# A two-layer hybrid decoder step: the next tile's input projections dealt over other steps of a slot, with second buffers for heads and turned x

## The reference, cut to what matters

```python
for each layer:
    xn = rmsnorm(x, norm_mix)
    (a_gate, a_x, b_q, b_k, b_v, b_qi, b_ki, b_wi, c_q, c_k, c_v, c_g, c_a) = split_cols(xn @ w_in)   # 2644 columns
    y_a = rglru_mixer(a_gate, a_x, ...)               # convolution of 4, gates, linear recurrence over rows
    q, k = rope(rmsnorm(b_q)), rope(rmsnorm(b_k))     # 8 query heads, 4 key heads of 64
    y_b = sparse attention: index scores from b_qi, b_ki, b_wi; the best 256 keys of each row; softmax over these
    y_c = gla_mixer(c_q, c_k, c_v, c_g, c_a, ...)     # gated linear attention with a state S
    x = x + concat(y_a, y_b, y_c) @ w_out
    x = x + square(relu(rmsnorm(x, norm_mlp) @ w_up)) @ w_down
```

## Time and profile before

| what | value |
|---|---|
| time, median of 3 runs | 4064.79 us (4063.27 to 4065.57) |
| span of the profiled execution (the page gives no other time for it) | 4072.7 us |
| busy in the span: PE, DVE, ACT, POOL | 88%, 52%, 25%, 12% |
| granted PE clock, mean | 0.89 of full speed |
| prompt mixer, layer 0 | about 36 to 990 us |
| prompt mixer, layer 1 | about 2057 to 3010 us |

### The profile page before, as it was taken

One profiled execution on the slowest core, in us unless ns is written; L12 is line 12 of the kernel. 1 busy time (PEld: TensorE's weight loads), 2 busy tenths in 40 slices (PEclk: granted clock), 3 DMA queues, 4 the chain that ended last, 5 costly groups with the idle time before them and its releaser, 6 DMA issues.

```text
span 4072.7 us, 52249 instructions
## 1 busy us (share of the span) xinstructions
PE 3569.3 (88%) x17850; PEld 2698.7 (66%) x17850; DVE 2124.8 (52%) x4881; ACT 1018.2 (25%) x2269; POOL 474.9 (12%) x637
## 2 busy tenths in 40 slices
PE   5778778888799999999987787787787999999999
PEld 3545555556447999999855554555464489999997
DVE  1347778877523444434323577887773334343344
ACT  2232333233401111111123233333234011111110
POOL 0100000221301000000001000002122000000000
PEclk9888888775999999999998888876768999999999
DMA  4000000237621111111410000002465201111111
GB/s 137 15 21 14 14 11 9 46 56 140 208 80 52 42 42 42 54 51 42 140 46 22 14 14 14 11 14 60 41 173 183 88 32 57 48 42 42 42 42 55
DMA packets 189759, 229.61 MB, mean 56 GB/s; under 512 B 72723, under 2 KB 150613, under 8 KB 189493
## 3 DMA queue, kind: packets, MB, share of 16 engines
q1 hardware_dynamic: 161796, 165.17, 15.1%
q0 software_dynamic: 20416, 50.27, 3.9%
q10 hardware_dynamic: 7280, 10.83, 0.8%
HBM read 203.22 MB, written 22.98 MB: 56 GB/s over the span
## 4 chain that ended last, share of the span: by engine, by line
PE 74%; DVE 10%; issue 5%; ACT 5%; DVEq 2%; SPq 1%; DMA 1%; POOLq 1%; POOL 1%; ACTq 0%
PE bank L1389 13%; PE bank L1390 13%; PE bank L1391 13%; PE bank L1096 10%; PE bank L1382 6%; PE bank L1092 5%; PE bank L1194 4%; DVE arena L1454 2%; ACT arena L709 2%; PE bank L1178 2%; DVE arena L1721 1%; PE bank L1186 1%; PE bank L1307 1%; PE bank L1140 1%; SPq L464 1%
## 5 line engine op out<-in xcount | busy, mean ns | idle before, releaser
L1861 DVE TENSOR_TENSOR x_rows<-x_rows,bank 128x512 f32<-128x512 f32 (+1 forms) x576 | 396.1, 688 | 632.1 <-PE bank L1391 632.1
L1096 PE MATMUL bank<-arena 128*128 128x512 f32 (+5 forms) x1440 | 526.5, 521 | 3.0 <-ACT arena L737 1.5
L1454 DVE TENSOR_SCALAR_CACHE_REDUCE arena<-arena,vectors 128x384 bf16<-128x384 f32 (+7 forms) x434 | 500.0, 1152 | 47.5 <-POOLq L406 15.3
L709 ACT ACTIVATE arena<-bank 128x512 f32<-128x512 f32 (+11 forms) x848 | 325.1, 440 | 772.3 <-PE bank L1096 334.0
L1389 PE MATMUL bank<-xT_hi,w_up_hi 128*128 128x364 f32 (+1 forms) x1536 | 506.0, 329 | 5.3 <-DVE vectors L1842 5.3
L1391 PE MATMUL bank<-xT_hi,w_up_lo 128*128 128x364 f32 (+1 forms) x1536 | 506.0, 329 | 0.0
L1390 PE MATMUL bank<-xT_lo,w_up_hi 128*128 128x364 f32 (+1 forms) x1536 | 505.9, 329 | 0.0
L1389 PE MATMUL bank<-w_down_hi,hidden_hi 128*128 128x512 f32 x1152 | 449.5, 390 | 7.5 <-issue 7.5
L1390 PE MATMUL bank<-w_down_lo,hidden_hi 128*128 128x512 f32 x1152 | 449.6, 390 | 0.0
L1391 PE MATMUL bank<-w_down_hi,hidden_lo 128*128 128x512 f32 x1152 | 449.6, 390 | 0.0
L1096 PEld LDWEIGHTS bank<-arena 128*128 128x128 f32 (+1 forms) x1440 | 254.5, 194 | 254.8 <-issue 226.4
(11 more groups left out here) (251 smaller groups left out, 4369.4 us busy)
## 6 DMA issues: line engine op xcount, KB each, us to landing
w_up_landing<-in_w_up SPq DMA_DIRECT2D x32, 1024.0 KB, 7.3
w_down_landing<-in_w_down SPq DMA_DIRECT2D x32, 1024.0 KB, 4.9
arena<-in_cache_k SPq DMA_DIRECT2D x160, 128.0 KB, 2.7
arena<-in_cache_v SPq DMA_DIRECT2D x160, 128.0 KB, 2.6
arena<-in_cache_v POOLq DMA_DIRECT2D x96, 128.0 KB, 3.1
arena<-in_cache_k POOLq DMA_DIRECT2D x96, 128.0 KB, 2.9
arena<-in_w_in ACTq DMA_DIRECT2D x4, 2048.0 KB, 16.1
out_projection<-in_w_out SPq DMA_DIRECT2D x16, 512.0 KB, 9.7
```

Source lines behind the costliest of these rows:

```text
L709: return act.activation(dst, src, ACT.Copy, scale=scale)
L1096: ins = mm(b[:R, o:o + w], xnT[:, c, 0:R], w_in[:, c, c0:c0 + w], start=c == 0, stop=c == 7)
L1454: ts(junk, sc, cf[:R].bitcast(F32), None, ALU.is_ge, ALU.add, accum_out=cnt[:R])
L1861: tt(x, x, b[P - R:P, :], ALU.add).then_inc(s_took, 1)
```

## The change

The turned x (`xnT`) and the heads (`hb`) get a second buffer each, used by odd tiles. The projections of tile `s+1` now stand in steps 0 (`G0`), 1 (`G2`), 2 (`G1`), 3 (`C0`), 6 (`C1`) and 8 (`G3`) of slot `s`, on PE and ACT; `x0`, `x1` move to step 7 of the slot before, for tile `s+2`, with tile 1's ahead of slot 0. The square of x (ACT) goes to step 4, its inverse root (POOL) behind the key stores, and `norm_x` (DVE, L1503) from step 1 to step 6, all for tile `s+2`. `G0` now waits for the key stores of the tile before last. The buffers take their room from POOL's descriptor scratch, which goes from 16384 to 4096 bytes per partition.

```diff
+LATER = {0: "G0", 1: "G2", 2: "G1", 3: "C0", 6: "C1"}
...
+        xnT1, hb1 = zone(SECOND0, ARENA, xnT1=(8, P), hb1=(18, 64))
+        xnTs, hbs = [xnT, xnT1], [hb, hb1]
...
                     elif PROJ[i] == "G0":
-                        if t:
-                            act.wait_ge(s_kst, T(l, t))
+                        if t >= 2:
+                            act.wait_ge(s_kst, T(l, t) - 1)
...
@@ scalar (ACT) @@
-                        if h == 0 and N_:
-                            square(s + 1)
+                        if h == 4 and s + 2 < TILES:
+                            square(s + 2)
...
-                        if h in (3, 4, 5) and N_:
-                            project(s + 1, h - 1)
...
+                        if h == 7 and s + 2 < TILES:
+                            project(s + 2, 0)
+                            project(s + 2, 1)
+                        if h in LATER and N_:
+                            project(s + 1, PROJ.index(LATER[h]))
                         if h >= 1 and A_ is not None:
                             probs_out(A_, h - 1)
...
@@ tensor (PE) @@
+                project(1, 0)
+                project(1, 1)
...
-                            if N_:
-                                project(s + 1, 0)
-                                project(s + 1, 1)
-                            if P_:
                                 gates(s)
...
+                        if h == 7 and s + 2 < TILES:
+                            project(s + 2, 0)
+                            project(s + 2, 1)
+                        if h in LATER and N_:
+                            project(s + 1, PROJ.index(LATER[h]))
...
@@ vector (DVE) @@
+                norm_x(1)
...
-                            if N_:
-                                norm_x(s + 1)
+                        if h == 6 and s + 2 < TILES:
+                            norm_x(s + 2)
...
@@ gpsimd (POOL) @@
                         stored(s_kst)
+                        if s + 2 < TILES:
+                            rstd(s + 2)
...
-    nc = _bacc.Bacc("TRN2", target_bir_lowering=False, num_devices=1)
+    nc = _bacc.Bacc("TRN2", target_bir_lowering=False, num_devices=1, dynamic_dma_scratch_size=4096)
```

More of the change, by code:

```diff
@@ L84, in plan @@
             if s == 0:
-                act += [(l, 0, n) for n in PROJ]
+                act += [(l, 0, n) for n in PROJ] + [(l, 1, "x0"), (l, 1, "x1")]
             for h in range(9):
@@ L212, in program @@
         ARENA = (53215 - const_cols - 288 - 16) // 8 * 8
+        SECOND0 = ARENA
+        ARENA += 8 * P + 18 * 64
         arena_at = (nc.sbuf_base + 31) // 32 * 32
@@ L617, in _ @@
                 rstd(0)
+                rstd(1)
                 for s in range(NST + 1):
@@ L728, in square @@
                         act.wait_ge(s_xn, TT3(l, 0, t))
-                    act.activation(xnT[:R].rearrange("p a b -> p (a b)"), xb[:R, :], ACT.Square, accum_out=small[:R, 15:16]).then_inc(s_ssq, 1)
+                    act.activation(xnTs[t % 2][:R].rearrange("p a b -> p (a b)"), xb[:R, :], ACT.Square, accum_out=small[:R, 15:16]).then_inc(s_ssq, 1)
                 def project(t, i):
-                    R = rows(t)
+                    R, hb = rows(t), hbs[t % 2]
                     if i < 2:
@@ L736, in project @@
                         for c in range(4):
-                            ins = act.activation(xnT[:, 4 * i + c, 0:R], b[:, c * R:(c + 1) * R], ACT.Identity, scale=gcol[:, 4 * i + c:4 * i + c + 1])
+                            ins = act.activation(xnTs[t % 2][:, 4 * i + c, 0:R], b[:, c * R:(c + 1) * R], ACT.Identity, scale=gcol[:, 4 * i + c:4 * i + c + 1])
                         ins.then_inc(s_evac, 1)
@@ L917, in _ @@
                     project(0, i)
+                    if i == 4:
+                        square(1)
+                project(1, 0)
+                project(1, 1)
                 for s in range(NST):
@@ L1091, in project @@
                             for c in range(8):
-                                ins = mm(b[:, m * R:(m + 1) * R], w_in[:, c, c0:c0 + P], xnT[:, c, 0:R], start=c == 0, stop=c == 7)
+                                ins = mm(b[:, m * R:(m + 1) * R], w_in[:, c, c0:c0 + P], xnTs[t % 2][:, c, 0:R], start=c == 0, stop=c == 7)
                     else:
@@ L1095, in project @@
                             for c in range(8):
-                                ins = mm(b[:R, o:o + w], xnT[:, c, 0:R], w_in[:, c, c0:c0 + w], start=c == 0, stop=c == 7)
+                                ins = mm(b[:R, o:o + w], xnTs[t % 2][:, c, 0:R], w_in[:, c, c0:c0 + w], start=c == 0, stop=c == 7)
                     ins.then_inc(s_full_a, 1)
                 def heads_T(t):
-                    R = rows(t)
+                    R, hb = rows(t), hbs[t % 2]
                     I = ident[:R, :R]
@@ L1253, in _ @@
                                 decay_logits(s)
-                            if N_:
-                                project(s + 1, 0)
-                                project(s + 1, 1)
-                            if P_:
                                 gates(s)
-                        if h in (3, 4, 5) and N_:
-                            project(s + 1, h - 1)
-                        if h == 6:
-                            if P_:
-                                gla_attention(s)
-                            if N_:
-                                project(s + 1, 5)
-                        if h == 7:
-                            if N_:
-                                project(s + 1, 6)
+                        if h == 6 and P_:
+                            gla_attention(s)
+                        if h == 7 and s + 2 < TILES:
+                            project(s + 2, 0)
+                            project(s + 2, 1)
+                        if h in LATER and N_:
+                            project(s + 1, PROJ.index(LATER[h]))
                         if h >= 1 and A_ is not None:
@@ L1505, in head_squares @@
                 def head_squares(t):
-                    R = rows(t)
-                    v.wait_ge(s_evac, A_AT[l, t, "G2"] + 1)
+                    R, hb = rows(t), hbs[t % 2]
+                    v.wait_ge(s_evac, max(A_AT[l, t, "G1"], A_AT[l, t, "G2"]) + 1)
                     tt(sq[:R], hb[:R, 0:12, :], hb[:R, 0:12, :], ALU.mult)
```

27 lines of the change are left out of this document (7 added, 20 removed).

## The result

The changed kernel is **slower**: 4162.9 us median (4148.4 to 4164.2, four runs) beside 4065.2 (4063.3 to 4069.5), ratio 1.0232, 95% interval 1.0215 to 1.0249. That is 98 us more; 47 less were forecast, and the time lies far outside the range. The profiled execution spans 4162.1 us, 89.4 more than the one profiled before.

A forecast was written before the change was run, and what follows sets the result against it. Early slots were taken as bound by PE, late ones by DVE. Terms summed to -23.2 us per layer, -46.4 for both, taking the profiled 4072.7 to 4026.3; less 7.9 to the median, 4018 us, range 3978 to 4050.

The forecast's parts named there:

- So 7.3 of the 10.2 to 12.3 us are filled and 3 to 5 stay.: PE's wait ahead of `heads_T`: `G0` put under it fills 7.3 us, and 3 to 5 us of waiting stay.
- The gate chain: Between `gates` and `gla_attention` in slots 0 and 1, fewer projections cover ACT and DVE: 5.3 us new PE idle time.
- Slot 0, +3.5: Slot 0, per layer: `G2` covers 3.8 us idle, against 5.3 us gate chain and about 2 us turning x: +3.5 us.
- Clock ... I take that as regained.: Slot 1: 6.3 us of work at the low clock cost 3.2 us more than at full clock, taken as regained.
- Slot 2 was put at 56 us of work at full clock and 14.3 idle.: Slot 2, per layer: PE's work plus idle time gives about 71 us, for 80 before: -8.7 us.
- `head_max(2)` and `head_max(3)` come 1.6 us later in slot 5: `G2` and `G1` ahead of values 0 and 1 delay DVE's row maxima: 1.6 us in slot 5, 2 in slot 3.
- 2.7 us behind the recurrence: Slot 5: `head_max(4)` waits 2.7 us behind the recurrence for `C0`'s evacuation, the probabilities' copy and head 2's values.
- What the late slots get back, 6.6 and 10.1 us: DVE's old waits, such as `gla_out` and index scores, go: 6.6 us in slot 5, 10.1 in slot 3.
- My worst end for the late slots: Slots 3 to 7, per layer: nothing given back and all new waits arising, +21.7 us.
- Slots 6 and 7 "at 0": Slots 6 and 7: no net change, the new waits growing with the keys and DVE's old ones not.
- The scratch at 0: POOL's smaller descriptor scratch costs 0; it would cost 1.85 us per page load if each waited for the landing before.
- slower, the wait behind the recurrence decides: Rival, 6%: `C0`'s evacuation stops values and DVE in slots 3 to 7, old waits stay: +10.7 us per layer, 4086 us.

The follow-up runs named there:

- experiment 11: The changed kernel with matmuls whose result nothing reads added on PE in slots 1 to 5, ahead of `heads_T` and some values: 4124.8 us, ratio 1.0146.
- C: The changed kernel with `G1`, `C0`, `G2`, `C1` in steps 4, 5, 6, 7 and only `G0` moved early, to step 0: 4015.1 us, ratio 0.9881.

## Why the prediction was wrong

Forecast were -23.2 us per layer; the profiles show +47 and +41. About 25 us of the error of each layer lie in slots 0 to 2, 49 and 39 in slots 3 to 7. Two steps failed: the price of work moved ahead of the values in the late slots, the larger part, and the clock taken as regained.

**"So 7.3 of the 10.2 to 12.3 us are filled and 3 to 5 stay."** Right: 3.81 in slot 1, 2.2 in slot 5, and `G0` moved alone is worth 21 us.

**The gate chain, 5.3 us new idle.** 7.05 in slot 1; the size was off by 1.7. The sum ran from the end of `C0`. ACT's logarithms, which stand behind the evacuation of `G1`, start it late: DVE's gate sums wait 7.0 us for them in slot 1, and only 3 us for the decays later. The kernels with `G1` in step 3 or 4 have 24 us of this wait in 8, as the kernel before, those with `G1` in step 2 41 to 44.

**Slot 0, +3.5.** +10. The 3.8 us of idle time that `G2` was to cover are still there, in another place: `G0` waits 3.72 us for the evacuation of `x1` (a table load of 1.28 us stands ahead of it on ACT). The gate chain adds 6.9, and PE is busy 3.2 us more.

**"Clock ... I take that as regained."** This step failed, and it stands under slots 1 and 2 both. In slot 1 PE's work was to fall by 3.2 us and went from 49.7 to 50.1, at 0.89 for 0.86. Slot 2 was put at 56 us of work at full clock and 14.3 idle. (That is 70.3; the sum took 71.3 and so -8.7, a slip of 1 us.) The idle time was nearly right, 16.0, in nine waits of up to 3.4 us in place of one of 10.2, one of 5.1 and small ones. The work took 69.0, at a granted clock of 0.78. By this account nearly all of the 13 us of the error in slot 2 are work at the low clock. But with the clock at 1.00 (experiment 11) the slot still took 78.4 us of 84.4, so only 6 are shown to come back with it. The Trainium skill, "TensorE: Matmul & The Clock Gate", section "A second HAM failure mode: psum-queue depth-cycling", reports of another kernel, in bf16, that short idle times of PE between groups of matmuls make its clock fall and rise again. The trace agrees in that the clock was 0.87 before and 0.78 after in slot 2. The page puts the loss between the groups; here it shows in the matmuls too, 9.38 us for `G2`.

**"`head_max(2)` and `head_max(3)` come 1.6 us later in slot 5", and 2.7 us behind the recurrence.** This is the step that weighed most. The mechanism was right, the three sizes were not: 4.77, 1.70 and 3.62 us, 10.1 for 4.3. `G2` was put at 6.2 us and takes 9.38. And the delay was not checked against a slack; that is only 2.5, 1.1 and 3.9 us in steps 1, 2 and 3 of C. Slots 3 to 7 were put at -12.2 us per layer and lost 36.4 and 27.2.

**What the late slots get back, 6.6 and 10.1 us.** The index wait went (2.9 to 0.6 in slot 5). The wait for `gla_out` did not: 4.7 us for 3.7. I had taken it that with `C1` in step 6 the queue would be free, but the values of head 6 ahead of it wait 7.5 us for ACT and run late. My worst end for the late slots was +21.7 us per layer.

**Slots 6 and 7 "at 0".** +12.7 and +6.1 us in layer 0, +5.4 and +6.0 in layer 1. The prediction let what is newly waited and what is given back cancel there, without a sum.

**The gain of 31 us from the second buffers and x turned two tiles ahead** was no term of the sum. It was luck in the forecast's favour: without it the miss would have been larger.

**The scratch at 0**: right, now measured. **The rival "slower, the wait behind the recurrence decides"** had the right sign, a chance of 6% and 4086 us. But `C0` in step 3, its mechanism, costs only 36 us; the two earlier moves, which it left as small costs in the late slots and gains in the early ones, cost 105 to 112. The single steps (-31 - 21 + 45 + 60 + 36) sum to 89 us, for 98 measured.

What stays open: how the loss divides among the maxima, the logarithms and PE's work at the low clock, since each feeds the next.

## What to carry to other kernels

An engine's idle time is room for work only if what stands behind it in the queues has slack. Before moving work into a gap, read how long ahead of its consumer each following result is ready, on the engine that bounds the stage, and compare that slack, not the gap, with the piece moved, priced at the clock that the rows show there. Try the moves of such a change one at a time: here one of four gained 21 us and the other three lost 141.

## What the runs showed of the hardware

With PE's one wait of 10 us in slot 2 turned into several of up to 3.4 us, the granted clock of the slot fell from 0.87 to 0.78, though PE's idle time fell by 3.6 us. The same projection `G2` took 6.21 and 6.32 us where the granted clock was 1.00 over its length, 6.95 at 0.89 and 9.38 at 0.67. Matmuls put into the gaps brought the clock of four slots to 0.94 to 1.00 and gained 38 us, while on C, where they ran longer than the gap, they cost 170. A quarter of the descriptor scratch made no difference to 96 loads each of K and V pages issued from POOL.
